# Four placements in a decoder layer: when three x tiles are loaded, and where a corner product, three LN tiles and the first spatial product stand

## The chip, the core and the metric

The kernel runs on one core of a Trainium2 chip. The metric is the device time of one execution in microseconds (us), the median of several runs. The core has five engines that run their own instruction streams in order and meet through semaphores: TensorE (PE, matrix products, with its weight loads PEld), VectorE (DVE), ScalarE (ACT), GpSimd (POOL) and SyncE (SP, which only issues DMAs here).

## The reference, cut to what is computed

```
z = rms_norm(x, g_pre) @ w_in            # 544 tokens (512 prompt, 32 sample), 1024 -> 3072
q, k, v, ga, u, vs, gg = split(z)        # 8 q heads, 4 k and v heads of 64; the others 512 wide
att = block-sparse causal attention      # prompt: two blocks of 256; sample: 1024 paged keys per sequence,
                                         # top 3 of 4 past blocks by q . mean(k), plus the own keys
v = group_layer_norm(gelu(vs), g_sgu)    # "LN": 8 groups of 64 channels
gm = gelu(u) * (tril(w_spatial[g]) @ v + b_spatial[g])   # in chunks of 128 positions
mix = concat(att * silu(ga), gm * silu(gg))
y = x + rms_norm(mix @ w_out, g_post)
```

Outputs are y for prompt and sample, the new K and V rows, and the sample's normalised v rows. All is float32; each product is made of three, from a high and a low part of both factors (w_hi, w_lo, act_hi, act_lo).

## The kernel before, in words

The input projection has 24 column tiles of w_in (q0 to q3, k0, k1, v0, v1, vs0 to vs3, u0 to u3, ga0 to ga3, gg0 to gg3). Each tile is done in two halves of the tokens, 256 and 288 wide, so there are 48 halves. Three matmul lines make one half: L1459 (w_hi by act_hi), L1460 (w_hi by act_lo), L1464 (w_lo by act_hi), eight of each. The first three halves have lines of their own (L1439, L1446, L1449). The results alternate between two PSUM banks, Z0 and Z1, that ScalarE or VectorE must read before the next half but one.

The order of everything else is written out by hand in `schedule()`: a list of steps, in which `after(h, step)` places a step behind half h. Every engine walks the same list and does its own share of each step, so one list sets the order on all of them. The steps that matter here:

- XT: the x tiles (five, of 128, 128, 128, 128 and 32 tokens) are squared by ScalarE (L801), scaled by VectorE (xn, L1040), turned by TensorE (L1404), copied as act_hi by ScalarE (L824) and their low part subtracted by VectorE (act_lo, L1059).
- WT and WB: w_spatial is turned, and WB makes from its corner, with a small matrix rep that VectorE copies (L1115), the block for the sample tokens (L1479, then VectorE's w_bd, L1120).
- DSC, DSM, DEX, DPT, DPV, DOD, DOT: decode attention in two rounds. DSM is a long chain of small VectorE operations (top-k; its last row is dstat, L1193), DEX eight exponentials on ScalarE (pd, L906), DPT eight turns of the probabilities pd by TensorE (in two banks), DOT the turn of the output, which VectorE copies into q_s (L1216).
- VSN tt: four turns of token tile tt of the gelu'd vs by TensorE (T<-zvs), mean and centring by VectorE (ln_mu L1225, vn L1227, which frees the bank), square by ScalarE (ln_sq L924), sum by VectorE (ln_var L1230).
- PSC, PN, PTR, PPV, ATT for each of 16 units of prompt attention: scores by TensorE (L1573, L1574, mask L1576), maximum on VectorE (nmax L1248), exponentials on ScalarE (L940), scaling on VectorE (probs L1258), turns by TensorE (L1377), high and low copies (ScalarE L952, VectorE pT_lo L1264), value products by TensorE (L1600), then sums into zga on VectorE (L1273, L1278).
- SP gp: spatial product of two channel groups by TensorE (L1610), VectorE's sp_sum (L1285, frees the bank) and zgg (L1289).

All turns and the WB, SP and DPT products share two PSUM banks T0 and T1 by turns: use n of a bank waits until use n - 2 has been read (`bank_free`). Weight tiles are loaded in pairs, split on ScalarE (w_hi, L796) and on GpSimd (L696) or VectorE (L1027).

Of the kernel before, what the change touches and what calls it, by code (L numbers as in the profile page):

```python
# [68 lines left out]
TILE_OF = {(kind, j): n for n, (kind, j, _) in enumerate(ORDER)}  # L69
# [7 lines left out]
UNITS = [(kvh, i) for kvh in range(KVH) for i in range(4)]  # L77
# [4 lines left out]
def schedule():  # L82

    s = [("XT", tt) for tt in range(TT)]
    side = {}

    def after(n, *steps):
        side.setdefault(n, []).extend(steps)


    for m, h in enumerate((3, 4, 5, 6, 10, 11, 12, 13, 15, 16, 17, 18, 21, 22, 23, 24)):
        after(h, ("KTR", m))
    after(6, ("WT",))
    after(7, ("WB",))
    after(9, ("DSC", 0), ("DSC", 1))
    after(12, ("KOW",))
    after(14, ("DSC", 2), ("DSC", 3), ("DOWN",))
    after(15, ("OWN",), ("DSM", 0))
    after(17, ("DEX", 0))
    after(16, ("KVN", 4), ("KVN", 0))  # L100
    for n, h in enumerate((17, 20, 22)):
        after(h, ("KVN", 1 + n))
    after(19, ("DPT", 0))
    after(20, ("DSC", 4), ("DSC", 5), ("DPV", 0, 0), ("DPV", 0, 1))
    after(22, ("DPV", 0, 2), ("DPV", 0, 3))
    after(24, ("DPV", 0, 4), ("DPV", 0, 5))
    after(28, ("DEX", 1))
    for n, h in enumerate((24, 25, 28, 29)):
        after(h, ("VSN", n))
    after(25, ("DSC", 6), ("DSC", 7), ("DPV", 0, 6), ("DPV", 0, 7))  # L110
    after(26, ("DOD", 0), ("DSM", 1))
    after(28, ("DOT", 0))
    after(30, ("DPT", 1))
    for pg in range(8):
        after(31 + pg // 2, ("DPV", 1, pg))
    after(31, ("VSN", 4))
    after(32, ("LN",))
    for n, tt in enumerate((4, 0, 1, 2, 3)):
        after(33 + 2 * n, ("LNM", tt))
    after(35, ("DOD", 1))  # L120
    after(36, ("DOT", 1))
    after(40, ("AS",))
    first = 30
    for h in range(first, 2 * NT):
        u = h - first
        if h in [2 * TILE_OF["gg", gp] + 3 for gp in range(3)]:
            after(h, ("SP", (h - 3) // 2 - TILE_OF["gg", 0]))
        if u < len(UNITS):
            after(h, ("PSC", u), ("PN", u))
        if 1 <= u < len(UNITS) + 1:  # L130
            after(h, ("PTR", u - 1))
        if 2 <= u < len(UNITS) + 2:
            after(h, ("PPV", u - 2))
        after(h, ("ZE", h // 2, h % 2))
        if 2 <= u < len(UNITS) + 2:
            after(h, ("ATT", u - 2))
    after(2 * NT - 2, ("MIX", 0, 0), ("MIX", 1, 0))
    for h, (n, half) in enumerate(HALF_ORDER):
        s.append(("Z", n, half))
        if h < first:  # L140
            s.append(("ZE", n, half))
        s += side.get(h, [])
    s += [("MIX", 0, 1), ("MIX", 1, 1), ("MIX", 2, 0), ("MIX", 2, 1), ("MIX", 3, 0), ("MIX", 3, 1)]
    s += [("SP", 3), ("SPS",), ("YS", 0), ("Y", 0), ("MIX", 4, 0), ("MIX", 4, 1), ("MIX", 5, 0), ("MIX", 5, 1),
          ("YS", 1), ("Y", 1), ("MIX", 6, 0), ("MIX", 6, 1), ("MIX", 7, 0), ("MIX", 7, 1),
          ("YF", 0), ("Y", 2), ("YS", 2), ("Y", 3), ("YS", 3), ("YH",), ("YF", 1)]
    s += [("Y2", tt) for tt in Y_ORDER]
    return s


SCHEDULE = schedule()


# [32 lines left out]
def lo_by(n):  # L186

    return "pool" if n in (0, 1, 2, 5, 6) or 13 <= n <= NT else "dve"
# [14 lines left out]
def lo_count(n):  # L203

    return sum(lo_by(m) == lo_by(n) for m in SPLIT_ORDER[:split_count(n)])
# [37 lines left out]
def build(nc, x_prompt, x_sample, cache_k, cache_v, page_table, g_pre, w_in, g_sgu, w_spatial,  # L243
# [13 lines left out]
    with ExitStack() as ctx:  # L257
        def sem(name):
            return ctx.enter_context(nc.semaphore(name))
# [150 lines left out]
        x_in = [sem(f"x_in{t}") for t in range(TT)]  # L410
# [24 lines left out]
        x_hi = sem("x_hi")  # L435
# [130 lines left out]
        def _(sp):  # L566
# [42 lines left out]
            def load_first(e):  # L609

                dst = w_raw[:, 0, :].rearrange("p (k c) -> p k c", k=KD)[:, :, e * P:(e + 1) * P]
                sp.dma_start(dst, w_in_v[:, :, e * P:(e + 1) * P]).then_inc(w_first[e], 16)

            page_ids = {}
            load_first(0)
            load_first(1)
            for tt in (2, 3, 4):
                sp.dma_start(x_sb[0:ROWS[tt], tt, :], x_src[tt]).then_inc(x_in[tt], 16)
            sp.dma_start(pages_i[:, :], page_table.rearrange("(o b) p -> o (b p)", o=1)).then_inc(pages_in, 16)
# [752 lines left out]
        def _(pe):  # L1372
# [20 lines left out]
            def turn_x(tt):  # L1393
                R = ROWS[tt]
                if tt == 2:
                    pe.wait_ge(x_split, 4)
                if tt == 3:
                    pe.wait_ge(x_split, 2)
                if tt == 4:
                    pe.wait_ge(xn_done, 2 * TT)  # L1400
                for kk in range(2):
                    pe.wait_ge(xn_done, 2 * tt + kk + 1)
                    for k in range(4):
                        last = nc.tensor.transpose(X_BANK[tt][kk][:, k * R:(k + 1) * R],  # L1404
                                                   xn[0:R, tt % 3, (4 * kk + k) * P:(4 * kk + k + 1) * P], ident[0:R, 0:R])
                    last.then_inc(xt_full, 1)
                    if tt < 2:
                        busy(WARM[3] if (tt, kk) == (1, 1) else WARM[2])
# [11 lines left out]
            for s in SCHEDULE:  # L1420
                kind, n = s[0], T_OF[s]
# [3 lines left out]
                elif kind == "Z":  # L1425
                    t, half = s[1], s[2]
                    h = HALF_AT[t, half]
# [4 lines left out]
                    if h < 3:  # L1432

                        pe.wait_ge(w_hi_done, t + 1)
                        pe.wait_ge(x_hi, 4)
                        if h == 2:
                            pe.wait_ge(xn_done, 2 * TT)
                        for k in range(KD):
                            mm(out, wh[:, k, :], act_hi[:, k, cols], start=(k == 0), stop=False)  # L1439
                        if h == 1:  # L1440
                            turn_x(2)
                        if h == 2:
                            turn_x(4)
                        pe.wait_ge(x_split, 4)
                        for k in range(KD):
                            mm(out, wh[:, k, :], act_lo[:, k, cols], start=False, stop=False)  # L1446
                        pe.wait_ge(w_split[lo_by(t)], lo_count(t))
                        for k in range(KD):
                            last = mm(out, wl[:, k, :], act_hi[:, k, cols], start=False, stop=(k == KD - 1))  # L1449
                        last.then_inc(z_full, 1)  # L1450
                        if h == 1:
                            turn_x(3)
                        continue
# [36 lines left out]
                elif kind == "DSC":  # L1490
                    u = s[1]
# [68 lines left out]
                elif kind == "PSC":  # L1560
                    u = s[1]
# [15 lines left out]
                elif kind == "PTR":  # L1577
                    u = s[1]
# [6 lines left out]
                elif kind == "PPV":  # L1585
                    u = s[1]
# [16 lines left out]
                elif kind == "SP":  # L1603
                    gp = s[1]
# [7 lines left out]
                elif kind == "SPS":  # L1612
                    bank_free(pe, n)
                    pe.wait_ge(t_free["dve"], freed(T_FREED_BY, T_OF["WB",])[1])
                    for g in range(GRP):
                        e, gp = g % 2, g // 2
# [79 lines left out]
```

## Time and profile before

| | |
|---|---|
| median of 3 runs (283.49, 283.56, 284.8) | 283.56 us |
| the profiled execution | 283.24 us, of which the span from first to last instruction is 281.5 |
| TensorE busy | 270.4 us (96% of the span) |
| VectorE busy | 197.4 us (70%) |
| ScalarE busy | 154.9 us (55%) |
| GpSimd busy | 81.5 us (29%) |
| granted TensorE clock, mean | 0.996 of full speed |
| DMA | 43.39 MB, 154 GB/s over the span |

Busy time is the union of an engine's instructions. Matmuls are pipelined and their ends are modelled, so a busy TensorE is not one at its peak, and an idle time before one of its rows is a little less than the wait. An engine that is not the bottleneck may be idle at no cost.

### The profile page before, as it was taken

To read this page: it belongs to the slowest core of one execution; us is meant where nothing else is said; L and a number is where in the kernel's file an instruction comes from. 1 tells how busy PE (TensorE), PEld (TensorE's weight loads), DVE (VectorE), ACT (ScalarE), POOL (GpSimd) and SP (SyncE) were. 2 spreads that over 40 slices of the span, in tenths; PEclk is the share of its full clock that TensorE was granted. 3 is DMA by queue.
4 is the path that set the end of the run, shared out by engine and by line. 5 is a ranking of instruction groups with operands and counts; after the bars stand their busy time and mean duration, and the time that the engine had idled before them with its cause. 6 is when DMAs were issued, how large, how long until landed. Compare 5 with 4: busy or idle time off the path is not lost.

```text
span 281.5 us, 6112 instructions
## 1 busy us (share of the span) xinstructions
PE 270.4 (96%) x2155; PEld 237.5 (84%) x2155; DVE 197.4 (70%) x451; ACT 154.9 (55%) x355; POOL 81.5 (29%) x96
## 2 busy tenths in 40 slices
PE   8999999999999999999899999999899999999992
PEld 3799988999997887998787999998798976767892
DVE  4786885699743525835558889899979894927773
ACT  5973667632692323288875556555374563628621
POOL 4676505210412142243044373333350510000000
PEclk9999999999999999999999999999999999999998
DMA  7989994379999969530572017021008404040043
GB/s 246 332 270 196 207 282 114 125 206 232 265 313 283 318 190 311 152 122 31 149 242 68 2 29 234 1 81 71 0 2 275 193 1 149 2 150 2 19 175 123
DMA packets 29922, 43.39 MB, mean 154 GB/s; under 512 B 2963, under 2 KB 22419, under 8 KB 29892
## 3 DMA queue, kind: packets, MB, share of 16 engines
q1 hardware_dynamic: 26226, 29.76, 37.2%
q0 software_dynamic: 3664, 13.24, 15.0%
q8 instruction: 17, 0.28, 0.5%
q14 instruction: 13, 0.11, 0.1%
q10 hardware_dynamic: 2, 0.00, 0.0%
HBM read 39.59 MB, written 3.41 MB: 153 GB/s over the span
## 4 chain that ended last, share of the span: by engine, by line
PE 72%; DVE 14%; ACT 9%; issue 3%; DVEq 0%; POOL 0%; ACTq 0%; POOLq 0%
PE Z L1459 11%; PE Z L1464 10%; PE Z L1460 10%; PE T L1377 3%; DVE probs L1258 3%; PE S L1501 3%; PE Z L1415 2%; DVE pT_lo L1264 2%; PE O L1600 2%; PE O L1536 2%; PE S L1415 2%; PE S L1416 2%; PE Z L1417 2%; PE S L1417 2%; PE Z L1416 2%
## 5 line engine op out<-in xcount | busy, mean ns | idle before, releaser
L1459 PE MATMUL Z<-act_hi,w_hi 128*128 128x288 f32 (+1 forms) x344 | 89.5, 293 | 0.4 <-ACT zvs L873 0.3
L1460 PE MATMUL Z<-act_lo,w_hi 128*128 128x288 f32 (+1 forms) x344 | 88.0, 288 | 0.0
L1459 PEld LDWEIGHTS Z<-act_hi,w_hi 128*128 128x128 f32 x344 | 64.8, 188 | 2.6 <-issue 1.6
L1460 PEld LDWEIGHTS Z<-act_lo,w_hi 128*128 128x128 f32 x344 | 64.8, 188 | 0.0
L696 POOL TENSOR_TENSOR w_lo<-w_raw,w_hi 128x1024 fp32r<-128x1024 f32 x16 | 38.2, 2388 | 54.4 <-ACT w_hi L796 54.4
L1464 PE MATMUL Z<-act_hi,w_lo 128*128 128x256 f32 (+1 forms) x336 | 49.0, 288 | 0.0
L1464 PEld LDWEIGHTS Z<-act_hi,w_lo 128*128 128x128 f32 x336 | 44.8, 188 | 0.0
L796 ACT ACTIVATE w_hi<-w_raw 128x1024 fp32r<-128x1024 f32 x32 | 33.5, 1051 | 15.0 <-DMA w_raw<-in_w_out 10.0
L940 ACT ACTIVATE probs<-S,nmax 128x128 f32<-128x128 f32 (+3 forms) x32 | 16.6, 524 | 23.9 <-DVE nmax L1248 22.5
L1027 DVE TENSOR_TENSOR w_lo<-w_raw,w_hi 128x1024 fp32r<-128x1024 f32 x15 | 18.1, 1209 | 16.0 <-ACT w_hi L796 16.0
L1135 DVE STREAM_TRANSPOSE kT<-k_ring 128x1024 f32<-128x1024 f32 x16 | 19.7, 1238 | 0.4 <-PE S L1501 0.2
L704 POOL DMA_DIRECT2D w_raw<-in_w_in x10 | 9.3, 928 | 33.2 <-DVE w_lo L1027 29.7
L1258 DVE TENSOR_SCALAR probs<-probs,rsum 128x128 f32<-128x128 f32 (+3 forms) x32 | 15.2, 475 | 1.1
L1248 DVE TENSOR_REDUCE nmax<-S 128x1 f32<-128x128 f32 (+3 forms) x32 | 14.1, 480 | 1.2 <-PE S L1576 1.1
L1264 DVE TENSOR_TENSOR pT_lo<-T,pT_hi 128x128 fp32r<-128x128 f32 (+3 forms) x32 | 14.1, 482 | 0.1
L1377 PE MATMUL T<-ident,probs 128*128 128x128 f32 x80 | 12.1, 276 | 2.1 <-DVE vn L1227 0.9
L952 ACT ACTIVATE pT_hi<-T 128x128 fp32r<-128x128 f32 (+3 forms) x32 | 12.2, 440 | 0.0
L768 POOL TENSOR_TENSOR vn<-vn,g_sgu_bc 128x512 f32<-128x512 f32 (+1 forms) x5 | 6.4, 1285 | 19.4 <-DVE vn L1240 19.4
L1600 PE MATMUL O<-pT_hi,v_st 128*128 128x256 f32 x40 | 11.5, 315 | 0.5 <-DVE zga L1278 0.5
L777 POOL TENSOR_TENSOR zu<-zu,zgg 128x544 f32<-128x544 f32 x4 | 5.4, 1352 | 22.0 <-DVE zgg L1106 22.0
L882 ACT ACTIVATE th<-Z 128x256 f32<-128x256 f32 (+1 forms) x16 | 6.4, 399 | 9.7 <-PE Z L1464 9.5
L1255 DVE RECIPROCAL rsum<-psums 128x1 f32<-128x1 f32 x32 | 5.1, 160 | 8.9 <-ACT probs L940 8.9
(272 smaller groups left out, 557.3 us busy)
## 6 DMA issues: line engine op xcount, KB each, us to landing
w_raw<-in_w_in POOLq DMA_DIRECT2D x10, 1024.0 KB, 7.0
k_ring<-in_cache_k SPq DMA_DIRECT2D x64, 128.0 KB, 4.7
v_ring<-in_cache_v SPq DMA_DIRECT2D x64, 128.0 KB, 4.0
w_raw<-in_w_out SPq DMA_DIRECT2D x8, 512.0 KB, 4.4
x_sb<-in_x_prompt SPq DMA_DIRECT2D x4, 512.0 KB, 5.6
x_res<-in_x_prompt SPq DMA_DIRECT2D x4, 512.0 KB, 5.2
out<-y_sb SPq DMA_DIRECT2D x8, 256.0 KB, 2.0
w_raw<-in_w_in SPq DMA_DIRECT2D x2, 512.0 KB, 6.5
```

The costliest lines, as they stand in the source:

```text
L696: nc.gpsimd.tensor_tensor(w_split_tile(False, n), w_tile(n), w_split_tile(True, n).bitcast(fp32), ALU.subtract)\
L796: nc.scalar.activation(w_split_tile(True, n), w_tile(n), ACT.Copy).then_inc(w_hi_done, 1)
L940: ins = nc.scalar.activation(probs[:, u % 2, g, 0:keys], S[:, g * 512:g * 512 + keys], ACT.Exp, bias=nmax[:, u % 2, g:g + 1], accum_out=ps ...
L1027: nc.vector.tensor_tensor(w_split_tile(False, n), w_tile(n), w_split_tile(True, n).bitcast(fp32), ALU.subtract)\
L1135: nc.vector.transpose(kT[:, m // 2 % 2, m % 2, :, :, :].rearrange("p q a j -> p (q a j)"), k_slot(m).rearrange("p q c -> p (q c)")).then_i ...
L1258: nc.vector.tensor_scalar(part, part, rsum[:, u % 2, g:g + 1], 0.5, ALU.mult, ALU.mult).then_inc(p_norm, 1)
L1264: nc.vector.tensor_tensor(pT_lo[:, u % 2, 0:blocks, g, :], T[(n + g) % 2][:, 0:blocks * P].rearrange("p (j q) -> p j q", q=P), pT_hi[:, u ...
L1377: return nc.tensor.transpose(T[n % 2][0:out_rows, col:col + rows], in_, ident[0:rows, 0:rows])
L1459: mm(out, wh[:, k, :], act_hi[:, k, cols], start=(k == 0), stop=False)
L1460: mm(out, wh[:, k, :], act_lo[:, k, cols], start=False, stop=False)
L1464: last = mm(out, wl[:, k, :], act_hi[:, k, cols], start=False, stop=(k == KD - 1))
L1600: last = mm(O[o_bank(u)][:, 0:256], v_st[:, j, kvh, :], part[:, u % 2, j, :, :].rearrange("p g q -> p (g q)"), start=(j == 0 and e == 0), ...
```

## The change

The diff has five edits. On SP, the loads of x tiles 2, 3 and 4 wait until x tile 1 has landed. On TensorE, the first group of matmuls of halves 0 to 2 waits for act_hi in two steps: the first four matmuls for three copies, the other four for four. In the schedule, WB moves from half 7 to half 8; VSN 2, 3 and 4 move from halves 28, 29 and 31 to 27, 28 and 29; and at half 43, where SP 0 stood ahead of everything, the order becomes scores, SP 0, scaling, value products, turns.

```diff
@@ schedule()
-    after(7, ("WB",))
+    after(8, ("WB",))
...
-    for n, h in enumerate((24, 25, 28, 29)):
+    for n, h in enumerate((24, 25, 27, 28)):
         after(h, ("VSN", n))
...
-    after(31, ("VSN", 4))
+    after(29, ("VSN", 4))
...
-        if h in [2 * TILE_OF["gg", gp] + 3 for gp in range(3)]:
-            after(h, ("SP", (h - 3) // 2 - TILE_OF["gg", 0]))
-        if u < len(UNITS):
-            after(h, ("PSC", u), ("PN", u))
-        if 1 <= u < len(UNITS) + 1:
-            after(h, ("PTR", u - 1))
-        if 2 <= u < len(UNITS) + 2:
-            after(h, ("PPV", u - 2))
+        spread = [gp for gp in range(3) if h == 2 * TILE_OF["gg", gp] + 3]
+        if spread and spread != [0]:
+            after(h, ("SP", spread[0]))
+        if spread == [0]:
+            after(h, ("PSC", u), ("SP", 0), ("PN", u), ("PPV", u - 2), ("PTR", u - 1))
+        else:
+            if u < len(UNITS):
+                after(h, ("PSC", u), ("PN", u))
+            if 1 <= u < len(UNITS) + 1:
+                after(h, ("PTR", u - 1))
+            if 2 <= u < len(UNITS) + 2:
+                after(h, ("PPV", u - 2))
@@ SP
             load_first(0)
             load_first(1)
+            sp.wait_ge(x_in[1], 16)
             for tt in (2, 3, 4):
                 sp.dma_start(x_sb[0:ROWS[tt], tt, :], x_src[tt]).then_inc(x_in[tt], 16)
@@ TensorE, halves 0 to 2
-                        pe.wait_ge(x_hi, 4)
                         if h == 2:
                             pe.wait_ge(xn_done, 2 * TT)
                         for k in range(KD):
+                            if k % 4 == 0:
+                                pe.wait_ge(x_hi, 3 + k // 4)
                             mm(out, wh[:, k, :], act_hi[:, k, cols], start=(k == 0), stop=False)
```

On ScalarE, from the gelu of half 27 on (zu is the gelu'd u, ln_sq the square of a centred tile, pd the decode exponentials), before:

```order
L877 ACTIVATE zu<-Z 128x288
L796 ACTIVATE w_hi<-w_raw 128x1024
L877 ACTIVATE zu<-Z 128x256
L906 ACT_TABLE_LOAD
L906 ACTIVATE pd<-S,bbias 128x128 x8
L907 ACTIVATE p_own<-own_s,dstat 128x32
L924 ACTIVATE ln_sq<-vn 128x512
L877 ACT_TABLE_LOAD
L877 ACTIVATE zu<-Z 128x288
```

And the same place in the changed kernel (its line numbers are 5 higher here):

```order
L882 ACTIVATE zu<-Z 128x288
L929 ACTIVATE ln_sq<-vn 128x512
L801 ACTIVATE w_hi<-w_raw 128x1024
L882 ACTIVATE zu<-Z 128x256
L911 ACT_TABLE_LOAD
L911 ACTIVATE pd<-S,bbias 128x128 x8
L912 ACTIVATE p_own<-own_s,dstat 128x32
L929 ACTIVATE ln_sq<-vn 128x512
L882 ACT_TABLE_LOAD
L882 ACTIVATE zu<-Z 128x288
```

A square (that of token tile 2) now stands ahead of the weight copy and the gelu of half 28; the square behind the decode exponentials is that of tile 3.

On TensorE at half 43, from the last matmuls of that half to the next half, before:

```order
L1464 MATMUL Z<-act_hi,w_lo 128x288 x8
L1610 MATMUL T<-wspT,vn 64x128 x8
L1573 MATMUL S<-k_hi,q_st 128x256
...
L1576 MATMUL S<-causal,ident_h 128x128 x2
L1377 MATMUL T<-ident,probs 128x128 x2
L1600 MATMUL O<-pT_hi,v_st 128x256
...
L1600 MATMUL O<-pT_lo,v_st 128x256
L1459 MATMUL Z<-act_hi,w_hi 128x256
```

And in the changed kernel:

```order
L1470 MATMUL Z<-act_hi,w_lo 128x288 x8
L1579 MATMUL S<-k_hi,q_st 128x256
...
L1582 MATMUL S<-causal,ident_h 128x128 x2
L1616 MATMUL T<-wspT,vn 64x128 x8
L1606 MATMUL O<-pT_hi,v_st 128x256
...
L1606 MATMUL O<-pT_lo,v_st 128x256
L1382 MATMUL T<-ident,probs 128x128 x2
L1465 MATMUL Z<-act_hi,w_hi 128x256
```

The spatial product (wspT, vn) moved behind the scores, and the two turns of probabilities moved from ahead of the eight value products to behind them.

On VectorE at the same half, before:

```order
L1278 TENSOR_TENSOR zga<-zga,O 128x128
L1285 TENSOR_TENSOR sp_sum<-T,b_bc 128x512
L1289 SCALAR_TENSOR_TENSOR zgg<-sp_sum,zu 128x512
L1248 TENSOR_REDUCE nmax<-S 128x1 x2
L1255 RECIPROCAL rsum<-psums 128x1
```

And in the changed kernel:

```order
L1283 TENSOR_TENSOR zga<-zga,O 128x128
L1253 TENSOR_REDUCE nmax<-S 128x1 x2
L1290 TENSOR_TENSOR sp_sum<-T,b_bc 128x512
L1294 SCALAR_TENSOR_TENSOR zgg<-sp_sum,zu 128x512
L1260 RECIPROCAL rsum<-psums 128x1
```

The two maxima of the scores moved ahead of the spatial sum and its product.

## Rows read from the trace of the kernel before

**Rows 1.** Timeline, 9.4 to 12 us: start us, us, instruction, [idle before <-releaser].
```profile
9.43 1.07 ACT L824 ACTIVATE act_hi<-O 128x512 fp32r<-128x512 f32 x2
10.05 1.29 DVE L1059 TENSOR_TENSOR act_lo<-O,act_hi 128x512 fp32r<-128x512 f32 x2
10.65 1.18 PE L1439 MATMUL Z<-act_hi,w_hi 128*128 128x256 f32 x8 [0.54 <-ACT act_hi L824]
11.34 1.07 ACT L801 ACTIVATE x_sq<-x_sb 128x1024 f32<-128x1024 f32 x1
11.68 0.52 PE L1446 MATMUL Z<-act_lo,w_hi 128*128 128x256 f32 x3
```
**Rows 2.** DMA view, packets that started between 5 and 8 us.
```profile
DMA packets 1866, 0.95 MB, mean 317 GB/s; under 512 B 20, under 2 KB 1864, under 8 KB 1866
```
**Rows 3.** Timeline of SP, from 2.8 us.
```profile
2.83 2.70 SPq L618 DMA_DIRECT2D x_sb<-in_x_prompt  x1
```
**Rows 4.** DMA view, issues between 2.6 and 5 us: KB each, us to landing.
```profile
x_sb<-in_x_prompt SPq DMA_DIRECT2D x1, 512.0 KB, 8.0
```
**Rows 5.** Timeline, 37 to 48 us, and TensorE's alone from 37.5.
```profile
37.19 1.21 PE L1464 MATMUL Z<-act_hi,w_lo 128*128 128x288 f32 x8
37.32 1.08 PE L1464 MATMUL Z<-act_hi,w_lo 128*128 128x288 f32 x7
38.63 0.17 DVE L1115 COPY rep<-ident 4x32 f32<-4x32 f32 x1
38.90 0.21 PE L1479 MATMUL T<-wspT,rep 4*32 4x32 f32 x2 [0.50 <-issue]
...
46.45 1.73 DVE L1089 TENSOR_TENSOR k_lo<-Z,k_hi 64x256 fp32r<-64x256 f32 x4 [0.49 <-ACT k_hi L862]
```
**Rows 6.** Timeline, 117 to 137 us; PEld is TensorE's weight load.
```profile
118.27 1.05 ACT L796 ACTIVATE w_hi<-w_raw 128x1024 fp32r<-128x1024 f32 x1
118.74 0.16 DVE L1193 TENSOR_REDUCE dstat<-four 128x1 f32<-128x4 f32 x1
...
120.80 0.38 ACT L877 ACTIVATE zu<-Z 128x256 f32<-128x256 f32 x1 [1.48 <-PE Z L1464]
121.24 0.69 DVE L1225 TENSOR_REDUCE ln_mu<-T 128x8 f32<-128x512 f32 x1 [2.34 <-PE T L1377]
121.96 0.69 DVE L1227 SCALAR_TENSOR_TENSOR vn<-ln_mu,T 128x512 f32<-128x512 f32 x1
...
124.72 0.68 ACT L924 ACTIVATE ln_sq<-vn 128x512 f32<-128x512 f32 x1
126.03 0.84 DVE L1216 COPY q_s<-T 64x32 f32<-64x32 f32 x4
...
128.37 0.42 PEld L1377 LDWEIGHTS T<-ident,pd 128*128 128x128 f32 x4 [0.32 <-DVE vn L1227]
```
**Rows 7.** Timelines of TensorE, 133.8 to 136.4 and 148 to 149 us.
```profile
136.09 0.30 PE L1377 MATMUL T<-ident,probs 128*128 128x128 f32 x1 [0.85 <-DVE vn L1227]
...
148.55 0.36 PE L1600 MATMUL O<-pT_hi,v_st 128*128 128x256 f32 x1 [0.46 <-DVE zga L1278]
```
**Rows 8.** Timeline, 196 to 205 us.
```profile
197.33 2.40 POOL L696 TENSOR_TENSOR w_lo<-w_raw,w_hi 128x1024 fp32r<-128x1024 f32 x1
...
197.91 1.90 DVE L1258 TENSOR_SCALAR probs<-probs,rsum 128x128 f32<-128x128 f32 x1
...
200.86 1.09 PE L1610 MATMUL T<-wspT,vn 128*64 128x128 f32 x16 [0.60 <-DVE pT_lo L1264]
...
202.63 0.68 DVE L1285 TENSOR_TENSOR sp_sum<-T,b_bc 128x512 f32<-128x512 f32 x1
...
203.46 0.30 PE L1377 MATMUL T<-ident,probs 128*128 128x128 f32 x1 [0.60 <-DVE sp_sum L1285]
203.96 0.75 DVE L1248 TENSOR_REDUCE nmax<-S 128x1 f32<-128x256 f32 x2
```
**Rows 9.** The chain that ended last, 203 to 205 us.
```profile
203.76 1.01 PE O L1600 x8
```

## The prediction

> **What bounds the kernel now.** TensorE is busy nearly all of the span (the table above), so I read the view of its waits first, and then the timeline at each place that the diff touches. The waits view names only nine releasers for TensorE, none of them a DMA; each one that matters below has its row of the timeline. They are single events: the first products [rows 1], the corner product [rows 5], the turns of the decode probabilities and the first turn of scores [rows 6, 7], the value products [rows 7], the first spatial product [rows 8]. The last is at 203.46 us; from there to the end TensorE waits for nobody. Whatever is taken away in front of it should therefore reach the end. A row's end is modelled and a successor starts before it, so the idle time in a row is less than what the wait costs; where I can, I use distances between starts.
>
> **The x tiles 2 to 4 held back: 0.** Between 5 and 8 us the DMA view shows 1866 packets, 1864 of them under 2 KB; a row of x is 4 KB, so what moves then is the two weight tiles issued earlier, and x tile 2 stands behind them [rows 2]. Its issue blocked SP from 2.83 for 2.70 us anyway, to 5.53, and it landed 8.0 us after its start, at 10.83 [rows 3, 4]. Issued at about 5.6 it still joins a queue with weights to move until about 8, so it lands when it did; x tile 1, ahead of both, gains nothing. ScalarE begins on tile 2 at 11.34, 0.5 us after the landing [rows 1]. What follows on SP (tiles 3 and 4, the page table, a weight pair, the K pages) is issued some 0.5 us later into the same backlog. Bounds: 0, and a loss of 2.3 (rival 2).
>
> **The first weight tiles wait in two steps: 0.2.** ScalarE's two copies for x tile 1 run from 9.43 to 10.50, so the first is done at about 9.97. TensorE starts its eight matmuls at 10.65, 0.15 after the second [rows 1]. Now four of them start at 10.12 and the others at 10.65, so the group ends half a group, 0.5 us, earlier. Next are the products with the low parts, which need VectorE's second subtraction: 10.05 + 1.29 = 11.34 [rows 1]. They start 0.15 later, at 11.49, where they started at 11.68: 0.2 is left. Bounds 0 and 0.5.
>
> **The corner of w_spatial behind half 8: 0.6.** The last matmuls of half 7 start 0.13 apart (eight from 37.19, seven from 37.32), so the corner product could start at 38.24. It starts at 38.90, just after VectorE's small copy ended at 38.80, the last of a chain of small operations [rows 5]. Behind half 8 that copy is over 2 us old, and the wait of 0.66 goes. I take 0.6, since the step from a narrow to a wide matmul, a tenth, stays; the idle time in the row, 0.5, is the lower bound, 0.7 the upper. VectorE's mask product now stands between the subtractions of halves 8 and 9, where VectorE sat idle 0.49 [rows 5]; without that cover it would delay a bank that TensorE needs only a half later.
>
> **LN centring of tiles 2, 3 and 4 at halves 27, 28, 29: 0.2.** On the gaining side: TensorE stood idle 0.85 before 136.09, since a turn of scores needed the bank that VectorE frees with the centring of tile 4 [rows 7]. With tile 4 two halves earlier that wait goes, and tile 4's own four turns leave that place (four turns take 0.4, as in the row at 128.37 [rows 6]). On the losing side: ScalarE's square of a centred tile now stands in front of the next half's weight copy and gelu, and ScalarE works in order. Tile 2 is centred behind VectorE's long top-k chain, which ends at 118.90; the two operations take 122.65 - 121.24 = 1.41, so tile 2 is ready at 120.33 [rows 6]. ScalarE, which copied weights at 118.27, now idles until then, squares (0.68), copies weights (1.05, overlapping by 0.1 at each end) and does the gelu of 120.80 at about 121.85: 1.05 late [rows 6]. From there the order is that of before (exp table, exponentials, square), so VectorE, which waits for tile 3's square, makes its four copies of the decode output at 127.1 instead of 126.03. The centring of tile 4 is queued behind them: 127.1 + 0.84 + 1.41 = 129.35. The second four turns of the decode probabilities need exactly that bank. They started at 128.37 and now start at 129.4 [rows 6]. So TensorE loses 1.05 and gets 0.85 and 0.4 back: 0.2. At 148.55 it waits another 0.46 for VectorE's zga, which hangs on ScalarE's exponentials [rows 7]; by the same steps those begin 0.2 earlier, which lets the 0.2 through. Bounds: a gain of 1.3 if tile 4's bank comes in time; a loss of 0.6 if ScalarE is 1.8 late and not 1.05. GpSimd's weight subtraction (2.4 us, [rows 8]) follows the late weight copy and ends near 124.4, before the half in front of 128.37 uses it.
>
> **The first spatial product behind the scores: 0.4.** VectorE is late here: one multiplication of probabilities took 1.90 us. It began at 197.91, while GpSimd ran from 197.33 to 199.73, and ended at 199.81 [rows 8]. So TensorE stood idle 0.60 before the spatial product at 200.86 and 0.60 before 203.46, where a turn waited for sp_sum (202.63 + 0.68 = 203.31) [rows 8]. Now the scores fill the first wait. The product still starts at 200.86, the eight value products (1.01, [rows 9]) follow from 201.9, and the turns come last. On VectorE the two maxima (0.75) stand ahead of sp_sum and overlap it by a tenth, so it ends at 203.97; the second turn starts 0.15 later, near 204.1 [rows 8]. Before, the value products followed that turn; now they lie ahead of it, in its wait. The next half starts 1.01 - (204.1 - 203.46) = 0.4 earlier. VectorE keeps pace, as ScalarE's exponentials now run under the spatial sum. Bounds: 0, and 1.2 (both idle times).
>
> A rule bears on that 1.90. The Trainium skill, page "SBUF — State Buffer", section "SBUF: two separate sides", says that VectorE and GpSimd share a pair of ports under an exclusive lock, the later one blocking until the other's instruction is over; the trace agrees, with an end 0.08 us behind GpSimd's. By that rule it matters which VectorE operation starts inside a GpSimd one, and that is rival 3.
>
> **Sum.** 0 + 0.2 + 0.6 + 0.2 + 0.4 = 1.4 us. The profiled execution took 283.24 (a span of 281.5 and 1.7 around it), so 281.8. The median of the three runs is 283.56, 0.3 above it; as a median, 282.1. The rivals' times are medians too.
>
> **Rivals.**
> 1. The LN move loses. ScalarE is 1.8 late, and the wait amid the decode turns grows by the difference. For it: three engines hand the delay on there without slack. Against: each step is a row of before, moved. 1.4 - 0.8 = 0.6: 282.9.
> 2. The hold costs, and the kernel is slower. If the issue of x tile 2 again takes 2.70 us after the wait, it ends at 8.3 and the tile lands 2.8 late, near 13.6; 0.5 of that is slack, and TensorE has nothing else to do in the other 2.3: 283.56 - 1.4 + 2.3 = 284.4. It decides from a landing about 0.9 late (the 0.5, and an estimated 0.4 in TensorE's own order). Against: SP came free just when tile 1 had landed.
> 3. The lock falls elsewhere. A multiplication of scores that was clear of GpSimd's 2.4 us starts inside them and loses up to 2 us on VectorE; 283.56 - 1.4 + 2.0 = 284.2 at most, half of that more likely. Against: in that stretch all engines move alike.
> 4. More is gained. Tile 4's bank comes in time for the decode turns, and ScalarE's exponentials shorten the wait at 148.55: 0.9 more, 281.2. Against: the chain of rows above.
> 5. The gains in front of the scores come to nothing, as VectorE paces the stretch up to 204: only 0.4 stays, 283.2. Against: VectorE entered that stretch behind TensorE and has no clock of its own.
>
> **Chances and range.** The forecast 0.48, rival 1 0.20, rival 2 0.05, rival 3 0.06, rival 4 0.15, rival 5 0.06. Half a per cent, 1.4 us, is about what a measurement of this kernel can tell from no change, and the forecast lies on it. Of its 0.48 I put 0.31 on the faster side, with all of rival 4 and 0.02 of rival 1: faster 0.48; slower 0.05, from the worst of rivals 2 and 3; within, 0.47. The range takes in rivals 1 and 5 and reaches rival 4, leaving out some 0.18: 281.2 to 283.4. The forecast's own is 281.6 to 282.6.
>
> **What would show it.** TensorE's first matmuls in two groups from about 10.1, and the low products at 11.5. No wait at the corner product. From there on all times 0.8 earlier; with that taken off, a wait of some 0.9 amid the decode turns, none at the first turns of scores, and as long a one as now at the value products of 148.55. At the first spatial product scores in place of the wait, and a shorter wait at the last turn. The prediction is wrong if x tile 2 lands after 11.7, if ScalarE does not idle for the centred tile 2, or if TensorE waits anywhere behind the spatial product.

## The result and the profile after

| | before | changed |
|---|---|---|
| median | 283.76 us (10 runs, 283.49 to 285.42) | 281.74 us (10 runs, 281.37 to 283.06) |
| profiled execution | 283.24 us, span 281.5 | 281.37 us, span 279.6 |

The ratio is 0.9927, with a 95% interval of 0.9907 to 0.9947: 0.7% faster, 2.0 us between the medians and 1.9 us between the two profiled executions. The granted TensorE clock is 0.998 of full speed (0.996 before). Here and below, four executions that were recorded in a slower state are left out of the times: one of the kernel before (530.88 us) and one in each of three experiments (286.11, 289.17 and 284.55 us).

The page of the changed kernel, its first rows:

```profile
span 279.6 us, 6112 instructions
PE 270.5 (97%) x2155; PEld 237.7 (85%) x2155; DVE 197.1 (70%) x451; ACT 155.1 (55%) x355; POOL 81.4 (29%) x96
```

The busy times are those of before to within 0.3 us; 1.9 us of waiting has gone from the span. The view of TensorE's waits (what it waited for: us in total, times, longest) has six rows left where it had nine. Three of them:

```profile
...
PE T L1382 <- DVE sp_sum L1290: 0.9, 1, 0.9
PE T L1382 <- DVE pT_lo L1269: 0.6, 1, 0.6
PE T L1382 <- DVE vn L1232: 0.5, 1, 0.5
...
```

The first is at the first spatial product and the third amid the decode turns; the second, at 193.62 us, stood in the kernel before too, at 195.25 and as long.

To see where the time came from, I match each matmul with the same one of before and take the difference of their starts, TensorE's lead. It is told here where it changes, from the rows at hand.

**The front.** Timeline of 9 to 14 us:

```profile
9.41 1.08 ACT L829 ACTIVATE act_hi<-O 128x512 fp32r<-128x512 f32 x2
10.03 1.29 DVE L1064 TENSOR_TENSOR act_lo<-O,act_hi 128x512 fp32r<-128x512 f32 x2
10.14 1.17 PE L1445 MATMUL Z<-act_hi,w_hi 128*128 128x256 f32 x8
11.31 1.07 ACT L806 ACTIVATE x_sq<-x_sb 128x1024 f32<-128x1024 f32 x1
11.37 0.77 PEld L1452 LDWEIGHTS Z<-act_lo,w_hi 128*128 128x128 f32 x6 [0.26 <-DVE act_lo L1064]
...
13.19 1.06 ACT L806 ACTIVATE x_sq<-x_sb 128x1024 f32<-128x1024 f32 x1 [0.48 <-DMA x_sb<-in_x_prompt]
```

The first matmuls start at 10.14 instead of 10.65, the low products at 11.37 instead of 11.68 [rows 1]; the second of these still waits a little, and from it on the lead is 0.20 (0.16 from 22 us on). ScalarE takes up x tile 2 at 11.31, as before. SP issues x tiles 2 and 3 in 1.03 us together, where the issue of tile 2 alone took 2.70 [rows 3]. SP's timeline:

```profile
5.62 1.03 SPq L623 DMA_DIRECT2D x_sb<-in_x_prompt  x2
```

The DMA view, issues between 5.5 and 6.1 us, puts the landing of tile 2 5.4 us after its start (8.0 before [rows 4]), so at 11.0, 0.2 later than before:

```profile
x_sb<-in_x_prompt SPq DMA_DIRECT2D x1, 512.0 KB, 5.4
```

X tile 3 comes later: issued at 6.22 instead of 5.57, it lands at 13.2 instead of 12.6. ScalarE took it up at 12.63 before, and now waits 0.48 us for it, to 13.19. All that ScalarE does next moves with it, down to the high part of the third weight tile, which is done at 17.75 instead of 17.19. TensorE's first product with that tile starts at 17.89 (18.05 before), so of 0.86 us of slack there 0.14 is left: in this execution the delay costs nothing, but only just. How much of it is the hold's stays open, since tile 3 lands between 12.4 and 14.5 us over the traces, with and without the hold.

**The corner.** Timeline of TensorE, 37 to 41.4 us:

```profile
37.03 1.22 PE L1470 MATMUL Z<-act_hi,w_lo 128*128 128x288 f32 x8
38.08 0.28 PE L1465 MATMUL Z<-act_hi,w_hi 128*128 128x256 f32 x1
...
40.98 0.24 PE L1485 MATMUL T<-wspT,rep 4*32 4x32 f32 x2
...
41.40 0.29 PE L1466 MATMUL Z<-act_lo,w_hi 128*128 128x288 f32 x1
```

Half 8 follows half 7 with no wait, and the lead jumps to 1.07. The corner product then stands behind half 8 without a wait, but its narrow matmuls and the step into the wide ones take 0.36 back (1.07 to 0.71 at 41.40). At 58 us the lead is 0.63.

**The LN move.** ScalarE, VectorE and TensorE, from their timelines of 117 to 137 us:

```profile
119.63 0.63 ACT L929 ACTIVATE ln_sq<-vn 128x512 f32<-128x512 f32 x1 [1.89 <-DVE vn L1232]
121.12 0.36 ACT L882 ACTIVATE zu<-Z 128x256 f32<-128x256 f32 x1
125.02 0.68 ACT L929 ACTIVATE ln_sq<-vn 128x512 f32<-128x512 f32 x1
125.74 0.69 DVE L1235 TENSOR_REDUCE ln_var<-ln_sq 128x8 f32<-128x512 f32 x1 [3.27 <-ACT ln_sq L929]
126.34 0.84 DVE L1221 COPY q_s<-T 64x32 f32<-64x32 f32 x4
127.93 0.67 DVE L1232 SCALAR_TENSOR_TENSOR vn<-ln_mu,T 32x512 f32<-32x512 f32 x1
128.66 0.66 PE L1382 MATMUL T<-ident,pd 128*128 128x128 f32 x4 [0.54 <-DVE vn L1232]
...
134.89 0.39 PE L1382 MATMUL T<-ident,probs 128*128 128x128 f32 x2
136.27 0.48 ACT L945 ACTIVATE probs<-S,nmax 128x256 f32<-128x256 f32 x1
```

From the kernel before, the first turn of scores and ScalarE's rows behind it:

```profile
134.96 0.28 PE L1377 MATMUL T<-ident,probs 128*128 128x128 f32 x1
135.97 0.63 ACT L924 ACTIVATE ln_sq<-vn 32x512 f32<-32x512 f32 x1 [1.31 <-DVE vn L1227]
137.92 0.48 ACT L940 ACTIVATE probs<-S,nmax 128x256 f32<-128x256 f32 x1
```

ScalarE waits 1.89 us for the centred tile 2, and its gelu runs at 121.12; VectorE's sum for tile 3 waits 3.27 us and holds up the four copies and the centring of tile 4, for which the second decode turns wait. At the scores of 134.19 the lead has fallen from 0.63 to 0.08. At the first turns of scores there is no wait where 0.85 us stood [rows 7]: the lead is 1.17 right behind them. And the value products, which waited 0.46 idle at 148.55 [rows 7], start without an idle time in their row:

```profile
146.14 0.83 PE L1382 MATMUL T<-ident,probs 128*128 128x128 f32 x6
146.91 0.36 PE L1606 MATMUL O<-pT_hi,v_st 128*128 128x256 f32 x1
```

The lead there is 148.55 - 146.91 = 1.64. The move has given 1.64 - 0.63 = 1.0 us.

**The first spatial product.** Timelines of 196 to 203 us:

```profile
195.71 2.39 POOL L701 TENSOR_TENSOR w_lo<-w_raw,w_hi 128x1024 fp32r<-128x1024 f32 x1
196.29 1.89 DVE L1263 TENSOR_SCALAR probs<-probs,rsum 128x128 f32<-128x128 f32 x1
...
201.00 0.75 DVE L1253 TENSOR_REDUCE nmax<-S 128x1 f32<-128x256 f32 x2
201.66 0.68 DVE L1290 TENSOR_TENSOR sp_sum<-T,b_bc 128x512 f32<-128x512 f32 x1
...
202.49 0.30 PE L1382 MATMUL T<-ident,probs 128*128 128x128 f32 x1 [0.91 <-DVE sp_sum L1290]
202.62 0.36 PE L1465 MATMUL Z<-act_hi,w_hi 128*128 128x256 f32 x1
```

The two waits of 0.60 [rows 8] have become one of 0.91; in the next half the lead is 1.91, and it stays at 1.9 to the end: 0.2 + 0.4 + 1.0 + 0.3 = 1.9. VectorE's long multiplication still falls inside the same subtraction of GpSimd: it runs from 196.29 to 198.18, 0.08 us past the subtraction's end at 198.10.

### The profile page after: what moved, and what is told of

The parts are those of the page before. It is cut to its first block, busy times and chain, and to the rows that moved or that the text cites. A ratio compares the mean times of both kernels' runs of the same rounds, so it can differ in the third digit from the quotient of the medians.

```text
span 279.6 us, 6112 instructions
## 1 busy us (share of the span) xinstructions
PE 270.5 (97%) x2155; PEld 237.7 (85%) x2155; DVE 197.1 (70%) x451; ACT 155.1 (55%) x355; POOL 81.4 (29%) x96
## 4 chain that ended last, share of the span: by engine, by line
PE 71%; DVE 16%; ACT 7%; issue 4%; DMA 1%; DVEq 0%; ACTq 0%
PE Z L1465 11%; PE Z L1470 10%; PE Z L1466 10%; PE T L1382 3%; DVE probs L1263 3%; PE O L1542 3%; PE S L1507 3%; PE Z L1420 2%; DVE pT_lo L1269 2%; PE S L1420 2%; PE S L1421 2%; PE Z L1422 2%; PE S L1422 2%; PE Z L1421 2%; PE O L1606 2%
## 5 line engine op out<-in xcount | busy, mean ns | idle before, releaser
L1032 DVE TENSOR_TENSOR w_lo<-w_raw,w_hi 128x1024 fp32r<-128x1024 f32 x15 | 18.1, 1214 | 16.0 <-ACT w_hi L801 16.0
```

What stands on the lines that cost most here:

```text
L1032: nc.vector.tensor_tensor(w_split_tile(False, n), w_tile(n), w_split_tile(True, n).bitcast(fp32), ALU.subtract)\
```

## The experiments

Twelve runs, in three groups of four that each ran on one chip beside the kernel before; the changed kernel itself ran again in the second group only. Executions of one kernel scatter by up to nearly 4 us upwards from a sharp lower edge, so beside the median I give the lowest time. The kernel before had a median of 284.1 to 284.2 us in all three groups and a lowest of 283.2 to 283.4. Even so, one and the same kernel (the last of these experiments) has medians of 280.37 and 281.29 in two groups, with lowest times of 280.15 and 280.03. So medians that differ by less than about 1 us settle nothing, and what an edit does is read from the traces.

**The LN move alone**, on the kernel before:

```
-    for n, h in enumerate((24, 25, 28, 29)):
+    for n, h in enumerate((24, 25, 27, 28)):
-    after(31, ("VSN", 4))
+    after(29, ("VSN", 4))
```

> The kernel before with the LN centring move alone. Theory A (the move is worth more than the 0.2 of the prediction, since tile 4's square no longer stands in front of ScalarE's exponentials): near 134 us TensorE is 0.4 to 0.6 us behind the kernel before, the 1.02 us at the first turn of scores and the 0.62 us at the value products (starts against starts) are both gone, and from there it leads by 0.9 to 1.1 us: 282.7 to 282.9 us. Theory B (the wait at the value products went because of what was gained in front, not because of the move): it stays at some 0.5 us here, the lead is 0.4 to 0.5 us, 283.3 us.

283.50 us median (before 284.23), ratio 0.9978, interval 0.9950 to 1.0006; lowest 282.47 against 283.36. The medians differ by 0.7 and the lowest by 0.9. The profiled execution is 0.92 us behind after its first 60 us, most of it (0.78) by 22 us, far ahead of the edit (the last section), so only what follows counts. TensorE's timeline:

```profile
136.41 0.39 PE L1377 MATMUL T<-ident,probs 128*128 128x128 f32 x2
...
147.66 0.83 PE L1377 MATMUL T<-ident,probs 128*128 128x128 f32 x6
148.41 0.36 PE L1600 MATMUL O<-pT_hi,v_st 128*128 128x256 f32 x1
```

Both waits are gone, and the lead goes from -0.92 (60 us) through -1.44 (135.71) to 0.14 (148.41): a loss of 0.5, then a gain of 1.6, a gain of 1.06 in all. Theory A holds, B falls: the wait at the value products goes with the move alone. The median does not tell A from B: it lies above both forecasts, nearer to B's 283.3, while the lowest time is 0.9 below, as A has it. What decides is the trace.

**Tile 4 put back**, in the changed kernel (its centring is behind half 31 again, tiles 2 and 3 stay moved):

```
-    after(29, ("VSN", 4))
+    after(31, ("VSN", 4))
```

> The changed kernel with the centring of tile 4 put back behind half 31; tiles 2 and 3 stay at 27 and 28. Theory A (the new wait amid the decode turns comes from tile 4's place in VectorE's queue, and both later waits from tile 4's centring and square): no wait of over 0.2 us amid the decode turns (0.70 in the changed kernel), the waits at the first turn of scores (about 1.0) and at the value products (0.4 to 0.6) are back, 0.8 to 0.9 us slower than the changed kernel: 282.5 to 282.7 us. Rival (ScalarE's square of tile 2, which holds up the weight copy, makes the decode wait): that wait stays near 0.7 us, and the time is about 283.3 us.

282.52 us (lowest 282.11), 0.8 to 0.9 above the medians of the changed kernel. The timelines of TensorE and ScalarE:

```profile
127.21 1.03 PE L1382 MATMUL T<-ident,pd 128*128 128x128 f32 x8
...
135.19 0.63 ACT L929 ACTIVATE ln_sq<-vn 32x512 f32<-32x512 f32 x1 [1.95 <-DVE vn L1232]
135.84 1.28 ACT L945 ACT_TABLE_LOAD   x1
137.14 0.48 ACT L945 ACTIVATE probs<-S,nmax 128x256 f32<-128x256 f32 x1
```

And its view of waits:

```profile
PE T L1382 <- DVE vn L1232: 0.9, 1, 0.9
PE O L1606 <- DVE zga L1283: 0.4, 1, 0.4
```

The eight decode turns run in one go, and both later waits are back, as theory A said; from 123 to 148 us TensorE loses 0.7 on the changed kernel. ScalarE's three rows show the link that the prediction missed: ScalarE waits 1.95 us for the centred tile 4, squares it, and only then loads its table for the exponentials of the scores.

**The sum of tile 3 late**, in the changed kernel (VectorE centres tile 4 before it sums the squares of tile 3):

```
-                    dve.wait_ge(sq_done, tt + 1)
-                    nc.vector.tensor_reduce(ln_var[0:R, tt, :], ln_sq[0:R, :].rearrange("p (g c) -> p g c", g=GRP), AX.X, ALU.add).then_inc(ssq_done, 1)
+                    for m in {3: (), 4: (3, 4)}.get(tt, (tt,)):
+                        dve.wait_ge(sq_done, m + 1)
+                        nc.vector.tensor_reduce(ln_var[0:ROWS[m], m, :], ln_sq[0:ROWS[m], :].rearrange("p (g c) -> p g c", g=GRP), AX.X, ALU.add)\
+                            .then_inc(ssq_done, 1)
```

> The changed kernel with VectorE's variance sum of tile 3 moved behind the centring of tile 4, so that VectorE does not stand in front of ScalarE's square before it centres tile 4. Theory A (the chain of exponentials, square, sum, copies of the decode output, centring is what the second four decode turns wait for): their wait of 0.70 us goes, and as ScalarE and VectorE are paced by TensorE there, 0.5 to 0.7 us reach the end: 281.0 to 281.2 us. Rival (ScalarE or VectorE paces the stretch from 130 to 147 us): the time taken away comes back as a wait at the value products near 147 us, and the time stays at 281.6 to 281.8 us.

280.82 us (lowest 280.52), ratio to before 0.9894, interval 0.9863 to 0.9925. VectorE and TensorE:

```profile
122.90 0.84 DVE L1221 COPY q_s<-T 64x32 f32<-64x32 f32 x4
126.11 0.67 DVE L1232 SCALAR_TENSOR_TENSOR vn<-ln_mu,T 32x512 f32<-32x512 f32 x1
126.71 0.67 DVE L1236 TENSOR_REDUCE ln_var<-ln_sq 128x8 f32<-128x512 f32 x1
128.03 1.03 PE L1384 MATMUL T<-ident,pd 128*128 128x128 f32 x8
```

The copies run 3.4 us earlier, tile 4 is centred by 126.78, and the decode turns, which had lost 0.70 us between starts, don't wait. No wait appears at the value products; TensorE even gains another 0.2 there, so the changed kernel had still lost a little at that place. With both, 0.9 us are gained on the changed kernel in the trace, more than the 0.5 to 0.7 that were expected, and the time is 0.2 below the expected range. This shows that the new decode wait hung on VectorE's sum, which stood in front of the copies and the centring, and that what is taken away there reaches the end.

**The spatial product put back in front of the scores**, in the changed kernel (its old order of half 43):

```
-        if spread and spread != [0]:
+        if spread:
```

> The changed kernel with the first spatial product put back in front of the scores. By the prediction's term the kernel loses 0.4 us (282.1 us); by the two traces, in which TensorE's lead grows from 1.62 to 1.91 us there, 0.3 us (282.0 us). Two waits of some 0.77 us (starts against starts) return in place of the one of 1.07 us.

281.98 us (lowest 281.86), against 281.58 to 281.74 (lowest 281.28 and 281.37) of the changed kernel in its two measurements. The two waits are back, in TensorE's timeline:

```profile
199.52 1.09 PE L1614 MATMUL T<-wspT,vn 128*64 128x128 f32 x16 [0.58 <-DVE pT_lo L1267]
202.12 0.30 PE L1380 MATMUL T<-ident,probs 128*128 128x128 f32 x1 [0.59 <-DVE sp_sum L1288]
```

Over this place TensorE falls another 0.2 to 0.3 us behind the changed kernel (from 0.30 to 0.56, and 0.52 to the end), so by the traces the order is worth 0.2 to 0.3. The times (0.2 to 0.4 between the medians, 0.5 to 0.6 between the lowest, in different groups) do not tell the two expectations apart.

**The changed kernel again**, as yardstick.

> The changed kernel once more, unaltered, as the yardstick for the three kernels beside it. 281.5 to 282.0 us, 1.8 to 2.2 us under the kernel before; TensorE's order of gains as in its first trace (about 0.5 at the corner, 1.0 over the LN move, 0.3 at the first spatial product), only the first 20 us differing by some tenths with the landing of the first weights.

281.58 us (lowest 281.28, highest 284.13). Its profiled execution took 282.28, 0.9 more than the first one; all of it arises by 18.84 us (0.95 behind the first trace), and from there to the end that distance changes by less than 0.1. The expectation had some tenths there.

**The hold undone**, in the changed kernel, and later **the hold alone** on the kernel before:

```
-            sp.wait_ge(x_in[1], 16)
```

> The changed kernel without the wait that holds x tiles 2 to 4 back. The prediction's term (0): x tile 2 lands within 0.3 us of its landing in the changed kernel, the time is within 0.2 us of it. Rival (the hold lets the first weights land sooner): the first two weight tiles land more than 0.3 us later than with the hold, TensorE's first products start later, 0.3 to 0.6 us slower. Other rival (the hold costs, as its backlog moves to the next weights): 0.2 to 0.5 us faster.

> The kernel before with the hold of x tiles 2 to 4 alone. By the prediction's term (0) its median is that of the kernel before, 284.1 us. Theory C (the hold takes nothing from the best execution but keeps the first 22 us from straggling; of the kernels so far, those with the hold have their median 0.1 to 0.45 us above their fastest run, those without it 0.7 to 1.0 us): the fastest run stays at 283.4 us and the median comes down by 0.3 to 0.6 us, to some 283.6 us.

Undone: 282.36 us (lowest 281.39) against 281.58 (281.28). Alone: 284.44 (283.43) against 284.08 (283.20). The medians contradict each other: the kernel without the hold is 0.8 slower in the one, the one with it 0.4 slower in the other. The lowest times say 0.1 and 0.2, in opposite directions too. In the trace of the kernel without the hold, x tile 2 lands at 11.0 (11.0 and 11.3 with it), and the first two weight tiles land at 7.4 and 9.1 us, sooner than in the two traces of the changed kernel (8.0 and 9.7, 8.3 and 10.0): the rival that the hold lets them land sooner is not borne out. Theory C, which I took from the spread of the first eight kernels, falls: the hold alone has its median 1.0 us above its lowest, and its median did not come down.

**The corner back behind half 7**, in the changed kernel:

```
-    after(8, ("WB",))
+    after(7, ("WB",))
```

> The changed kernel with the corner of w_spatial back behind half 7. By the prediction's term it loses 0.6 us. By the two traces it loses 0.5: the wait of 0.66 and 0.15 of narrow steps behind it come back, and 0.3 us of steps behind half 8 go (the lead there falls from 1.07 to 0.67 us). 282.2 to 282.4 us.

282.11 us (lowest 281.68): 0.53 and 0.40 more than the changed kernel beside it, near the 0.5 of the two traces and a little less than the term. Only its times are used here.

**The first matmuls in one step**, in the changed kernel:

```
+                        pe.wait_ge(x_hi, 4)
-                            if k % 4 == 0:
-                                pe.wait_ge(x_hi, 3 + k // 4)
```

> The changed kernel with the first matmuls waiting for both halves of x tile 1 at once. By the prediction's term it loses 0.2 us: 281.8 us, with the first matmuls in one group some 0.5 us later and the low products 0.2 us later. Rival (the gain is lost by 22 us, where TensorE waits for the next weight pair anyway): no difference of more than 0.1 us.

282.54 us (lowest 281.53). TensorE's first matmuls, and the first of the third weight tile:

```profile
10.66 1.19 PE L1444 MATMUL Z<-act_hi,w_hi 128*128 128x256 f32 x8 [0.54 <-ACT act_hi L829]
11.68 0.53 PE L1451 MATMUL Z<-act_lo,w_hi 128*128 128x256 f32 x3
...
19.26 0.98 PE L1444 MATMUL T<-act_hi,w_hi 128*128 128x256 f32 x6 [0.92 <-ACT w_hi L801]
```

Up to 17.3 us it is 0.2 behind the first trace of the changed kernel, as predicted. At 19.26 it waits for its next weights, and in such an execution the 0.2 would be lost in that wait, as the rival says; where the weights come in time, as in the first trace of the changed kernel, it stays. The median is 0.8 to 1.0 above those of the changed kernel, which neither expectation has; the lowest times differ by 0.2. Both compare different groups, so the times do not show the 0.2.

**The spatial sum first**, in the kernel with the late sum of tile 3 (on VectorE alone):

```
+VECTOR_ORDER = list(SCHEDULE)
+_at = VECTOR_ORDER.index(("SP", 0))
+VECTOR_ORDER[_at - 1:_at + 1] = [("SP", 0), VECTOR_ORDER[_at - 1], ("SPZ",)]
...
+                    if gp == 0:
+                        continue
...
+                elif kind == "SPZ":
+                    nc.vector.scalar_tensor_tensor(zgg[:, 0, 0:SEQ], sp_sum[:, :], 0.5, zu[:, 0, 0:SEQ], ALU.mult, ALU.mult).then_inc(sp_done, 1)
```

> The kernel with the late sum of tile 3, and in it, on VectorE at the first spatial product, the spatial sum in front of the two maxima of the scores and the product with it behind them. If the remaining wait of 1.07 us at the second turn there is for the sum's place in VectorE's queue, the sum starts 0.5 to 0.7 us earlier, and so does the turn: 0.4 to 0.6 us less than the kernel with the late sum alone, 280.3 us. Rival (the maxima, which start 0.7 us later, hold up the exponentials, and a turn of the next half waits instead): within 0.2 us of 280.8 us, with a new wait of 0.3 to 0.6 us near 205 us.

280.37 us (lowest 280.15), ratio to before 0.9875, interval 0.9837 to 0.9913. VectorE and TensorE:

```profile
200.71 0.68 DVE L1295 TENSOR_TENSOR sp_sum<-T,b_bc 128x512 f32<-128x512 f32 x1
201.31 0.75 DVE L1258 TENSOR_REDUCE nmax<-S 128x1 f32<-128x256 f32 x2
...
201.54 0.30 PE L1393 MATMUL T<-ident,probs 128*128 128x128 f32 x1 [0.24 <-DVE sp_sum L1295]
...
205.40 0.61 PE L1393 MATMUL T<-ident,probs 128*128 128x128 f32 x4
```

The wait falls from 0.91 to 0.24, and the turns of the next half, at 205.40, have no wait in front of them: the rival does not occur there. Of some 0.7 us that TensorE gains here, 0.2 is lost again at 216 us, at turns of a later half, and 0.5 reaches the end. The other 0.24 is not the sum's length alone: the sum starts at 200.71, as soon as VectorE is done with zga, while the product ended near 200.0.

**The same without the hold, and again with it:**

> The kernel with the late sum of tile 3 and the spatial sum first, without the hold of x tiles 2 to 4. Theory C: its fastest run is that of the same kernel with the hold (280.2 us), its median 0.4 to 0.8 us higher than with it (280.8 to 281.2 us). By the prediction's term (0): the same median, 280.4 us.

> The kernel with the late sum of tile 3 and the spatial sum first, with the hold, once more beside the one without it: 280.2 to 280.5 us.

Without: 281.29 us (lowest 280.04). With: 281.29 (lowest 280.03). Not the 280.2 to 280.5 expected as a median, in either; the lower edge is where it was. That settles theory C as fallen: the two are alike. Over its two groups the kernel with the late sum and the spatial sum first is 1.0 to 1.25% below the kernel before (ratios 0.9904 and 0.9875), and its lowest times are 1.1 to 1.3 us below those of the changed kernel.

## Why the prediction was right, and which term was off

The time came out 0.4 below the predicted median and inside the forecast's own range. The sum was 1.4 and the traces show 1.9. Four terms came by the predicted mechanism and within 0.2 of their size; the LN move gave 0.8 more than its term, most of it by a path that the prediction did not have. That the time still fell into a range 1.0 us wide is partly luck: the corner and the spatial product together gave some 0.3 less, and the median of before, from three runs, was 0.2 below that of ten. The three signs of being wrong did not show (tile 2 landed at 11.0, ScalarE idled 1.89 us for the centred tile 2, nothing waited behind the spatial product), but of the signs of being right one failed: the wait at the value products was to stay. (The wait amid the decode turns, foretold at 0.9, is 0.70 between starts.)

1. **Hold: 0.** Right for the time. SP came free in time, tile 2 landed at 11.02, ScalarE took it up when it did before. Not priced was a later tile 3, which in the first trace left 0.14 of the 0.86 us that ScalarE's next weight copy had in hand. Three pairs with and without the hold agree at their lower edge within some 0.2 us; a smaller effect is not settled, as the medians of two pairs contradict each other.
2. **First weight tiles in two steps: 0.2.** Right in size and place (10.14 and 11.37, predicted 10.12 and 11.49), shown by the lead of 0.20, and by the trace with the edit undone, 0.2 behind up to 17.3 us. That it is lost in executions whose next weights come late is argued, not measured.
3. **Corner: 0.6.** A little less, 0.4 to 0.5. The wait of 0.66 went; not priced was that the corner's narrow steps cost more between half 8 and half 9 than between 7 and 8 (0.36, against 0.25: of the 0.91 by which the lead rose from 0.16, 0.66 was the wait).
4. **LN move: 0.2.** This is the term that was off; it measured 1.0. Its loss was right: ScalarE idles for tile 2, and the second decode turns start at 128.66, which with the 0.63 of lead added back is 129.29 on the clock of before, against 129.4 predicted. The gain at the first turn of scores was 1.0 to 1.1 and not 0.85, since the prediction took the idle time of a row for the wait, while the starts around that row show 1.02 lost (134.96 to 136.09, less a step of 0.11). The step that failed is the last: "by the same steps those begin 0.2 earlier". I moved ScalarE's exponentials with TensorE alone. But the square of tile 4, for which ScalarE had waited 1.31 us, stood in front of them and had been moved away: they began at 136.27 where they had begun at 137.92, 1.65 earlier, at a place where TensorE led by 0.08. So the wait at the value products went, 0.5 us. Of the 0.8 that the term was off, this is 0.5; 0.2 is the first turn of scores, 0.1 a smaller loss in front. Putting tile 4 back returned the square, the late exponentials and both waits; the move alone removed both.
5. **First spatial product: 0.4.** Right, with 0.3 left of it: with 1.62 of lead added, the second turn starts at 204.11 and the next half at 204.24 (predicted 204.1, and 0.4 earlier than the 204.61 of before): 0.37 earlier; 0.07 is lost in the step to that half's second matmul.

Of the rivals, the fourth came half true: ScalarE's exponentials did shorten the wait at 148.55, but tile 4's bank did not come in time for the decode turns. Rival 1 did not occur, nor rival 2 (a landing 0.2 late, with 0.5 of slack), nor rival 5 (the lead in front of the spatial product arrived whole; "no clock of its own" can only mean that VectorE's pace there is set by what TensorE hands it). Rival 3 did not either: the 1.89 us multiplication is the one that took 1.90 before. The Trainium skill's page "SBUF — State Buffer", section "SBUF: two separate sides", says that GpSimd and certain operations of VectorE (in a two-port mode, or with two SBUF inputs) exclude each other at a shared pair of ports. The after trace agrees once more, with an end 0.08 us past GpSimd's; that it is not every operation of VectorE shows too, as 17 maxima of scores start and end inside operations of GpSimd.

## What to carry to other kernels

When an operation is moved, go through both of its places on every engine that carries a part of it: the prediction priced what tile 4's square does where it arrives and forgot what it had held up where it stood. An in-order engine that waits for another's result (here VectorE for a square) blocks all that is queued behind it, so such a sum is best placed behind the work that others wait for; moving it took away a wait of 0.7 us that the change had made. Price a wait by distances between starts, and expect a moved narrow operation to bring its steps along (0.36 us at the corner).

## What the runs showed that was not expected

The scatter between executions of one kernel shows itself in these traces in the first 22 us. The second weight pair lands between 15.7 and 18.8 us in the thirteen profiles that I compared, and TensorE's first product of the third weight tile starts anywhere from 17.9 to 19.9 us, in most of the late ones after an idle time of up to 0.92 us for the weights. From there on the distance between the two traces of the changed kernel changes by less than 0.1 us in 260. What makes the landing vary stays open: kernels with the hold (15.7 to 18.1) and without it (16.1 to 18.8) show it alike.
